# A fused two-block layer on one core: the last two expert steps written out, and the order of work at the seam behind them

## What is computed

```python
def _expert_ffn(xb, w_gu, b_gu, w_down, b_down):
    gu = xb @ w_gu + b_gu                      # 1024 -> 2048
    gate, up = gu[:, :D_EXPERT], gu[:, D_EXPERT:]
    gate = jnp.minimum(gate, SWIGLU_LIMIT)
    up = jnp.clip(up, -SWIGLU_LIMIT, SWIGLU_LIMIT)
    glu = gate * jax.nn.sigmoid(SWIGLU_ALPHA * gate)
    return ((up + 1.0) * glu) @ w_down + b_down   # 1024 -> 1024
...
x = _layernorm(DEEPNORM_ALPHA * x + moe_out + ple, ln2_g, ln2_b)
# second block
mod = c @ w_ada + b_ada
shift, scale, gate = jnp.split(mod, 3, axis=-1)
h = rmsnorm(x, norm_g) * (1.0 + scale) + shift
proj = h @ w_in          # V0, Q0, K0, V1, ... are its units of 512 columns
```

## Time and profile before

| what | value |
|---|---|
| median of three runs | 1740.6 us |
| the profiled execution | 1739.38 us, span 1737.6 us |
| TensorE busy (records) | 1700.8 us, 98% of the span |
| TensorE weight loads busy | 997.3 us, 57% |
| VectorE busy | 570.5 us, 33% |
| ScalarE busy | 261.1 us, 15% |
| chain that ended last | TensorE 91%, DMA 5%, VectorE 2%, ScalarE 1% |
| data moved | 540.46 MB, mean 311 GB/s |
| mean granted TensorE clock | 0.999 of 2.4 GHz |

### The profile page before, as it was taken

One profiled execution on the slowest core, in us unless ns is written; L12 is line 12 of the kernel. 1 busy time (PEld: TensorE's weight loads), 2 busy tenths in 40 slices (PEclk: granted clock), 3 DMA queues, 4 the chain that ended last, 5 costly groups with the idle time before them and its releaser, 6 DMA issues.

```text
span 1737.6 us, 24288 instructions
## 1 busy us (share of the span) xinstructions
PE 1700.8 (98%) x10121; PEld 997.3 (57%) x10121; DVE 570.5 (33%) x1070; ACT 261.1 (15%) x446; POOL 28.9 (2%) x42
## 2 busy tenths in 40 slices
PE   8999999999999999999999999999999989999998
PEld 7787888888643433333333333433333338998885
DVE  2784377454341111111111111111121235536603
ACT  0323115002011111101010101101010121112200
POOL 1000000100000000000000000000000000000000
PEclk9999999999999999999999999999999999999999
DMA  8564332545799999999999999999999995532331
GB/s 320 191 257 183 146 122 100 166 164 191 270 404 424 421 424 427 427 427 428 428 427 428 426 428 427 428 428 427 426 428 427 428 418 205 194 146 102 141 143 46
DMA packets 65257, 540.46 MB, mean 311 GB/s; under 512 B 5514, under 2 KB 14276, under 8 KB 35744
## 3 DMA queue, kind: packets, MB, share of 16 engines
q1 hardware_dynamic: 58464, 527.31, 74.0%
q10 hardware_dynamic: 4560, 5.90, 1.2%
q0 software_dynamic: 2160, 6.17, 1.1%
HBM read 533.57 MB, written 5.78 MB: 310 GB/s over the span
## 4 chain that ended last, share of the span: by engine, by line
PE 91%; DMA 5%; DVE 2%; ACT 1%; issue 1%; SPq 0%; DVEq 0%; ACTq 0%
PE small L1440 24%; PE small L1482 12%; PE proj L816 10%; PE proj L1590 6%; PE proj L1002 5%; DMA arena<-in_expert_w_gu 4%; PE proj L1666 4%; PE proj L1415 3%; PE small L1388 3%; PE small L1427 2%; PE small L1447 2%; PE small L1081 2%; PE small L837 2%; PE proj L826 2%; PE proj L1529 2%; PE small L1547 2%
## 5 line engine op out<-in xcount | busy, mean ns | idle before, releaser
L1440 PE MATMUL small<-arena 128*64 128x512 f32 x2048 | 447.1, 593 | 6.8 <-DMA arena<-in_expert_w_gu 4.3
L1440 PEld LDWEIGHTS small<-arena 128*64 128x64 f32 x2048 | 151.1, 137 | 287.4 <-issue 274.5
L1482 PE MATMUL small<-arena 128*64 128x512 f32 x1024 | 226.8, 595 | 8.6 <-ACT arena L1924 7.9
L2593 DVE TENSOR_SCALAR arena<-small 128x512 f32<-128x512 f32 x32 | 22.1, 692 | 544.3 <-PE small L1447 544.3
L816 PE MATMUL proj<-arena 128*128 128x256 f32 x832 | 183.2, 380 | 0.9 <-DMA arena<-in_w_in_first 0.9
L816 PEld LDWEIGHTS proj<-arena 128*128 128x128 f32 x832 | 157.0, 190 | 23.1 <-DMA arena<-in_w_in_first 1.3
L1482 PEld LDWEIGHTS small<-arena 128*64 128x64 f32 x1024 | 74.5, 137 | 138.8 <-issue 138.8
L1590 PE MATMUL proj<-arena 128*128 128x128 f32 x896 | 100.5, 275 | 0.5 <-ACT arena L1982 0.5
L1590 PEld LDWEIGHTS proj<-arena 128*128 128x128 f32 x896 | 100.3, 192 | 1.1 <-ACT arena L1982 0.7
L1749 ACT ACTIVATE arena<-proj 128x512 f32<-128x512 f32 (+2 forms) x76 | 43.7, 593 | 361.1 <-PE proj L816 118.4
L1920 ACT ACTIVATE arena<-arena 128x512 f32<-128x512 f32 x32 | 20.1, 629 | 495.0 <-DVE arena L2593 495.0
(11 more groups left out here) (455 smaller groups left out, 1576.6 us busy)
## 6 DMA issues: line engine op xcount, KB each, us to landing
arena<-in_expert_w_gu SPq DMA_DIRECT2D x128, 2048.0 KB, 20.6
arena<-in_expert_w_down SPq DMA_DIRECT2D x31, 2048.0 KB, 28.0
arena<-in_expert_w_down SPq DMA_DIRECT2D x33, 1536.0 KB, 30.3
arena<-in_w_in_first SPq DMA_DIRECT2D x20, 2048.0 KB, 8.5
arena<-in_w_in SPq DMA_DIRECT2D x16, 2048.0 KB, 7.3
arena<-in_expert_w_down SPq DMA_DIRECT2D x33, 512.0 KB, 19.8
arena<-in_w_ada SPq DMA_DIRECT2D x6, 2048.0 KB, 9.9
arena<-in_w_branch SPq DMA_DIRECT2D x4, 2048.0 KB, 8.2
```

The source lines that it names most:

```text
L1440: mm = pe.matmul(bank[CAP * half:CAP * half + CAP, :], XG[:, k % 4, k // 4, :], w[:, k % 4, n * D + half * W:n * D + half * W + W], start= ...
L1482: mm = pe.matmul(y_bank[CAP * half:CAP * half + CAP, :], HM[:, m, u, :], w[:, half * W:half * W + W], start=u == 0 and m == 0, stop=u == 1 ...
```

## The change

The loop over expert steps ends two steps earlier on every engine, and its bounds n_steps - 2 and n_steps - 3 are computed into `total` and loaded into registers. The last two steps, a and b = a + 1 (30 and 31), are written out. SyncE issues both steps' gate/up weights, then both steps' down weights. TensorE does step a up to the turning of the rows, the gate/up product of b, the down product of a, turning of h of b, scatter of a, turning of b's slots, the down product of b. Step b has no gather and no turned rows. Its h is copied to the place of XG, its y is built in another bank.

At the seam "ada rows 5" moves from ahead of the first transposes to between H 0 and V0 0; "ada 4", "ada 5" and "gate8" move behind V0 1. The V0 weights are loaded in four pieces of 0.5 MB (chunks m and m + 4 of eight), each with a semaphore that V0 0 waits for piece by piece, and V0 0 sums its pairs in a slightly different nesting. ScalarE does the layer norm's root ahead of the copy of ada rows 4, and the copy of ada rows 5 behind the modulation of H 0. VectorE adds ada 4 and 5 behind the modulation of h 1. The helpers `gate_and_up`, `slots_turned`, `h_turned`, `down` hold what stood in TensorE's `expert_step`; the counts of unit semaphores are adapted to V0's own semaphores.

```diff
          + [f"Wb A {i}" for i in range(4)] + ["mix 0", "mix 1", "mix 2", "x1 0 0", "x1 0 1", "mix 3"]
          + ["logits 0", "x1 1 0", "x1 1 1", "logits 1", "rank", "gateT", "picked", "xg"]
-         + ["ada rows 4", "ada rows 5", "ada 4", "ada 5", "h 0", "h 1", "gate8"]
+         + ["ada rows 4", "h 0", "ada rows 5", "h 1", "ada 4", "ada 5", "gate8"]
          + [x for p in range(HEADS // 2) for x in [f"T {2 * p + odd} {b}" for odd in range(2) for b in range(3)] + [f"O {p}"]]
          + ["pool 0", "pool 1"]
          + [f"{n} {i}" for n in ("Wb2a", "Wb2p") for i in range(4)] + [f"mix2 {i}" for i in range(5)])
...
+            before_two = sp.value_load(total[0:1, 2:3], min_val=EXPERTS - 3, max_val=EXPERTS * T // CAP - 3)
@@ -699,9 +701,21 @@
                     expert_rows(3, u, half)
-            with sp.Fori(4, n_steps, 2) as i:
+            with sp.Fori(4, before_two + 1, 2) as i:
                 expert_block(i, False)
                 expert_block(i + 1, True)
+            for odd in range(2):
+                for u in range(2):
+                    for half in range(2):
+                        sp.wait_ge(sig("gu_used"), 4 * before_two + (4 * odd + 2 * u + half + 1))
+                        expert_rows(EXPERTS - 2 + odd, u, half)
+            for odd in range(2):
+                sp.wait_ge(sig("down_used"), before_two + odd)
+                down_first(EXPERTS - 2 + odd, odd)
+                sp.wait_ge(sig("y_full"), before_two + odd)
+                down_second(EXPERTS - 2 + odd, odd, slice(0, 3))
+                sp.wait_ge(sig("y_full"), before_two + (odd + 1))
+                down_second(EXPERTS - 2 + odd, odd, slice(3, 4))
             for i in range(2):
                 sp.wait_ge(sig("gu_used"), 4 * n_steps)
                 half = ins["w_ada_2"][0, :, (4 + i) * W:(5 + i) * W]
...
@@ -717,6 +731,10 @@
+                if n == 0:
+                    for m in range(4):
+                        sp.dma_start(weights2(name)[:, m::4, :], unit2_source(name)[0][:, m::4, :]).then_inc(sig(f"first_in_{m}"), 16)
+                    continue
                 sp.dma_start(weights2(name), unit2_source(name)[0]).then_inc(sig(f"unit2_in_{n % 3}"), 16)
...
                     mm = pe.matmul(x_bank[:, 0:P], XT[:, k, j * P:j * P + P], PLEW[:, k, bass.ds((i % 8) * P, P)], start=k == 0, stop=k == KD - 1)
                 mm.then_inc(sig("ple_full"), 1)
 
-            def expert_step(i, tile, odd, before=None):
...
@@ -1457,33 +1511,14 @@
                 if tile is not None:
                     pe.wait_ge(sig("ple_sig"), i - 7)
                 gather(x_bank).then_inc(sig("gathered"), 1)
-                pe.wait_ge(sig("pickw_ready"), i + 1)
-                for j in range(TT):
-                    mm = pe.transpose(y_bank[:, j * P:j * P + P], PICKW[:, j, :], ident)
-                mm.then_inc(sig("ptw_full"), 1)
-                pe.wait_ge(sig("h_ready"), i + 1)
-                for m in range(4):
-                    mm = pe.transpose(gate_bank[:, m * P:m * P + P], GH.rearrange("s (p k) -> s p k", k=4)[:, :, m], ident)
-                mm.then_inc(sig("ht_full"), 1)
+                slots_turned(i, y_bank)
+                h_turned(i)
                 pe.wait_ge(sig("rows_ready"), i + 1)
                 turn_rows(up_bank).then_inc(sig("rows_turned"), 1)
-                pe.wait_ge(sig("ptw_ready"), i + 2)
-                pe.wait_ge(sig("hm_ready"), i + 1)
-                for u in range(2):
-                    if odd:
-                        pe.wait_ge(sig(f"odd_in_{2 + u}"), 16 * i + 16 if u else 8 * i + 24)
...
-                    for m in range(4):
-                        w = expert_room(2 + u)[:, m, :]
-                        if odd and 4 * u + m < 7:
-                            w = extra[:, m, :] if u else more[:, m, :]
-                        for half in range(2):
...
@@ -1504,11 +1539,25 @@
+            before_last = pe.value_load(total[0:1, 1:2], min_val=EXPERTS - 2, max_val=EXPERTS * T // CAP - 2)
             two_steps(24, 26, None)
             pe.wait_ge(sig("ple_mul"), 18)
             for j in range(TT):
                 expert_bias(j)
-            two_steps(26, n_steps, None)
+            two_steps(26, before_last, None)
+            a, b = before_last, before_last + 1
+            expert_step(a, None, False, down_now=False)
+            pe.wait_ge(sig("hm_ready"), a + 1)
+            gate_and_up(b)
+            pe.wait_ge(sig("ptw_ready"), a + 2)
+            down(a, False, y_bank, HM)
+            h_turned(b)
+            pe.wait_ge(sig("y_ready"), b)
+            scatter()
+            slots_turned(b, up_bank)
+            pe.wait_ge(sig("hm_ready"), b + 1)
+            down(b, True, x_bank, HM_LAST)
+            pe.wait_ge(sig("ptw_ready"), b + 2)
             pe.wait_ge(sig("last_y_ready"), 1)
             for j in range(TT):
                 scatter((j,), counted=True)
...
-            pe.wait_ge(sig("seam_ready"), 1)
-            for i in range(2):
+            def ada_rows2(i):
+
...
+            pe.wait_ge(sig("seam_ready"), 1)
+            ada_rows2(0)
+            pe.wait_ge(sig("seam_ready"), 2)
+            w = weights2("V0")
+            for j in range(TT):
+                pe.wait_ge(sig("x2n_done"), j + 1)
+                for ps, lo, full_ in ((small(f"h {j}"), 0, "small_full"), (proj(f"H {j}"), 4, "proj_full")):
+                    for m in range(4):
+                        mm = pe.transpose(ps[:, m * P:m * P + P], base[:, j, (lo + m) * P:(lo + m + 1) * P], ident)
+                    mm.then_inc(sig(full_), 1)
+                if j == 0:
+                    ada_rows2(1)
+                ps = proj(f"V0 {j}")
+                for m in range(4):
+                    if j == 0:
+                        pe.wait_ge(sig(f"first_in_{m}"), 48)
+                    for k, piece in ((m, "h_low"), (4 + m, "h_high")):
+                        pe.wait_ge(sig(piece), 4 * j + m + 1)
+                        mm = pe.matmul(ps[:, :], HT[:, k, j * P:j * P + P], w[:, k, :], start=m == 0 and k == 0, stop=m == 3 and k > 3)
+                mm.then_inc(sig("proj_full"), 1)
             pe.wait_ge(sig("small_out"), small_no("ada rows 5") + 1)
             for i in range(2):
                 ps = small(f"ada {4 + i}")
                 for m in range(4):
                     mm = pe.matmul(ps[:, m:m + 1], ADAROW2[:, i, m * P:m * P + P], SEL2, start=True, stop=True)
                 mm.then_inc(sig("small_full"), 1)
-            pe.wait_ge(sig("seam_ready"), 2)
-            for j in range(TT):
-                pe.wait_ge(sig("x2n_done"), j + 1)
-                for ps, lo, full_ in ((small(f"h {j}"), 0, "small_full"), (proj(f"H {j}"), 4, "proj_full")):
-                    for m in range(4):
-                        mm = pe.transpose(ps[:, m * P:m * P + P], base[:, j, (lo + m) * P:(lo + m + 1) * P], ident)
-                    mm.then_inc(sig(full_), 1)
-                if j == 1:
-                    pe.wait_ge(sig("small_out"), small_no("ada 5") + 1)
-                    pe.transpose(small("gate8")[0:8, 0:P], MODT[:, 16:24], ident).then_inc(sig("small_full"), 1)
-                w = unit2("V0")
...
+            pe.wait_ge(sig("small_out"), small_no("ada 5") + 1)
+            pe.transpose(small("gate8")[0:8, 0:P], MODT[:, 16:24], ident).then_inc(sig("small_full"), 1)
...
@@ -1937,8 +2004,15 @@
                 expert_step(i, True)
             act.wait_ge(sig("total_ready"), 1)
             n_steps = act.value_load(total[0:1, 0:1], min_val=EXPERTS, max_val=EXPERTS * T // CAP)
-            with act.Fori(24, n_steps) as i:
+            before_last = act.value_load(total[0:1, 1:2], min_val=EXPERTS - 2, max_val=EXPERTS * T // CAP - 2)
+            with act.Fori(24, before_last) as i:
                 expert_step(i, False)
+            a, b = before_last, before_last + 1
+            expert_step(a, False, down_now=False)
+            sigmoid_of_gate(b)
+            y_copied(a, y_bank)
+            h_copied(b, HM_LAST)
+            y_copied(b, x_bank)
             act.wait_ge(sig("y_ready"), n_steps)
             act.nop().then_inc(sig("last_y_ready"), 1)
...
@@ -1962,14 +2036,15 @@
+                act.wait_ge(sig("small_out"), n)
                 act.activation(ADAROW2[:, i, :], small_bank[n % 4][:, :], ACT.Copy).then_inc(sig("small_out"), 1)
 
             log_and_exp()
+            rsqrt(rs2[:, 0:1], "ln2_var", "ln2_rstd", 1)
             ada_rows2(0)
-            rsqrt(rs2[:, 0:1], "ln2_var", "ln2_rstd", 1)
-            ada_rows2(1)
             squares_of_x2(0)
             modulated(0)
+            ada_rows2(1)
             rsqrt(rs2[:, 1:2], "ln2_var", "ln2_rstd", 2)
             squares_of_x2(1)
...
@@ -2573,7 +2650,7 @@
-                dve.wait_ge(sig("gathered"), i + 1)
-                pick(PICK, nxt, "pick_ready", False)
+                if not last:
+                    dve.wait_ge(sig("gathered"), i + 1)
...
```

(21 more changed lines are left out.)

82 lines of the change are left out of this document (57 added, 25 removed).

## The result

| | before | changed |
|---|---|---|
| median (range) of eight runs each, same chip, us | 1739.76 (1738.69 to 1742.21) | 1746.54 (1745.22 to 1750.49) |
| ratio changed / before, with its 95% interval | | 1.0041 [1.0032, 1.0050] |
| profiled execution, us | 1739.38 | 1750.49 |
| its span, us; mean granted clock | 1737.6; 0.999 | 1748.7; 0.993 |
| start of the run of Q0, K0 and the rest | 1447.58 | 1451.64 |

The profiled execution was the slowest of its eight. It already lies 2.0 us behind at the expert bias of step 30 (1378.06, before 1376.07), and its first expert step has a gate/up product of 15.65 us instead of 13.95, under a low clock; whether that is all of the 2.0 us is not shown.

A forecast was written before the change was run, and what follows sets the result against it. TensorE, busy 98% of the span, was taken as the bound, with loads setting the pace near the loop's end. Terms -3.6 + 1.4 + 2.4 + 3.9 = +4.1 us gave 1744.7 as a median; range 1741.5 to 1748.5.

The forecast's parts named there:

- rival 1: Seam: new 3.85 us idleness before the run's third product brings a second low clock, +1.5, in all +5.6, 1746.2; 17%.
- the case that I held likeliest: Whole kernel: the forecast itself, slower by +3 to +5 us, with 52%.
- Part 1: Last two expert steps: load waits, a gather and transposes go, so the last down product ends 3.6 us sooner.
- I take it as unbroken: Expert loop's end: the load stream has no gap near 1372, with 8 us in hand.
- the down weights of 31 end at 1411.7 as before: Step 31: reordered transfers leave the landing time of its down weights unchanged.
- Rival 2: Step 31: the down product follows the last landing, -6.6 instead of -3.6, sum +1.1, 1741.7; 9%.
- Part 2: Seam's first half: "ada rows 5" moves from idle time onto the path, +1.4 net.
- the -0.2 for the root: Seam: taking the layer norm's root ahead of the ada copy starts the first transposes 0.2 us sooner.
- Part 3: Seam's second half: columns and gate row on the path, +2.4; third product waits for VectorE's sums, +3.9.
- the V0 pieces cost nothing: Seam: cutting the V0 load is worth nothing, as its weights land before V0 is wanted.
- The second register load: Expert loop: a second register load on each engine costs nothing, falling before 1372 where TensorE has time to lose.
- Rival 3: Seam: the low clock falls wholly into the first idle time, so the sum is +2.7, 1743.3; 14%.

The follow-up runs named there:

- changed_again: The changed kernel run once more with no edit: 1748.0 us, 1.0041 of the kernel before.
- Experiment 7: Changed kernel with the last 0.5 MB of step 31's down weights loaded to a free place without waiting: 1747.54 us, 1.0042 of the kernel before.
- columns_behind: Changed kernel with ada 4 and 5 columns behind the run's second product and the gate row behind its first unit: 1740.74 us, 1.0004 of the kernel before.
- filler_both: Changed kernel with 20 identity products ahead of the first transposes and 16 ahead of the run's third product: 1744.46 us, 1.0020 of the kernel before.
- experiment 6: Changed kernel with V0's weights in one load instead of four pieces: 1750.12 us, 1.0049 of the kernel before.
- experiment 3: The same run as columns_behind: changed kernel with columns and gate row moved behind the run's first products, 1740.74 us.
- rows5_ahead: Changed kernel with "ada rows 5" back ahead of the first transposes and its copy ahead of the squares: 1748.46 us, 1.0045 of the kernel before.
- experiment 1: The same run as loop_alone: only the last two expert steps changed, the seam as before, 1740.81 us.
- kept_busy: Changed kernel with Experiment 7's load, ada 4 columns and 14 identity products before the transposes, ada 5 and gate row behind units 0 and 1: 1737.82 us.
- loop_alone: Changed kernel with everything behind the expert loop undone, so only the last two steps differ from before: 1740.81 us, 1.0004 of the kernel before.
- experiment 12: Kernel before the change with four identity products ahead of the first transposes: 1739.51 us, 0.9995 of the kernel before.
- v0_in_one: The same run as experiment 6: changed kernel with V0's weights in one load, 1750.12 us.

## Why the prediction was right in sign and short in size

The sign and the range held (1746.5 within 1741.5 to 1748.5); the difference was +6.8 where +4.1 was forecast. What came about is rival 1, at 17%, whose time was 1746.2, and not the case that I held likeliest. That 1746.2 and 1746.5 nearly agree is luck in part. The forecast was added to 1740.6, the median of three runs, and eight runs gave 1739.8; as a difference rival 1 said +5.6, and the medians say +6.8 to +7.4, the profile of `changed_again` +8.6. No miss made up for another: every term of the sum came out as forecast or worse.

**Part 1, -3.6, measured -2.5 to -2.8.** The removed waits, the gather and the transposes went as counted, and "I take it as unbroken" held: the stream ran at 429 and 433 GB/s in 1365 to 1375, and the last gate/up quarter landed at 1392.1, forecast 1392.0. In `changed_again`, 0.10 us later than before at the bias, three small terms were off by 0.8 together. Gate/up of 31 started at 1383.37, 0.15 later than counted; the down product of step 30 took 7.41 us instead of 7.09, waiting for weights where I had no wait (0.77 us in one piece in the other profile); the last half waited 0.52, where I counted 0.2. The step that failed is "the down weights of 31 end at 1411.7 as before". SyncE may issue their last 0.5 MB only when step 30's down product has ended, and the change moves that end behind the gate/up product of step 31: from 1389.9 to 1405.7. SyncE waits 26.6 us for it, the piece lands 7.1 us behind its issue, at 1412.8, and the stream runs at 328 GB/s in 1405 to 1410, before at 400. Experiment 7, in which that piece does not wait, had 408 and 387 GB/s and no wait in the last product; its 0.3 to 0.5 us are within the noise of the times. Rival 2 is out: the product started behind TensorE's own work, and only its second half waited for a load.

**Part 2, +1.4, measured +2.3.** The mechanism is the predicted one and one length was off. The clock was low from the first transposes to the end of "ada rows 5" instead of for 3.0 us: 3.49 us for that product (3.64 in the other profile) where I counted 2.5. Of the -0.2 for the root 0.1 came: the transposes start 10.0 us behind the last down product, before 10.1. In `columns_behind`, where the low stretch was short, the term was +1.4; in `filler_both`, where there was none, -0.2. I had written down that the longer idle time could lengthen the stretch, as an addition to rival 1, and left it out of the sum. That the V0 pieces cost nothing is in line with experiment 6. The second register load was not tried by itself; in `changed_again` the bias of step 30 stands 0.1 us later than before.

**Part 3, +2.4 and +3.9, measured +6.3.** Both terms came as worked out: 3.88 us idle where 3.85 were forecast, ended by VectorE's weight sums, and experiment 3 takes them away together by moving the columns in the queues. This part carries the result: without the wait and the low clock behind it (experiment 3, where the 1.84 us of the columns stay) the change measures 1740.7, no different from before.

**Rival 1.** I priced the second stretch at +1.5 from the length of the old one; it was +2.7 to +2.9, since it was about twice as long: the clock rose again at some 1462.3 in `changed_again` and 1465.0 in the other profile, so 5.3 and 5.6 us of work ran at half speed. I gave it 17% because the trace showed an idle 1.57 us without a fall. That row was 2.5 times shorter than the gap in question, and the idle times of the old seam, shorter still, had brought one. The Trainium skill, "TensorE: Matmul & The Clock Gate", section "Why this matters for your kernels", made rival 1 the likelier outcome; the runs agree: behind the seam's unfilled idle times of 3.5 us and more work ran at low clock in every profile (in `rows5_ahead` from some 0.5 us behind it on), and behind the filled ones at 1.00. It ran at low clock behind some shorter ones too: 1.11 us in the kernel before, 2.44 and 2.25 us in `rows5_ahead`. Why it did is not shown.

**Rival 3** (the low stretch falls into the idle time) came in no profile.

**What the gain came to.** The loop's end is worth 2.5 to 2.8 us at its own end and nothing that the times show by itself (experiment 1), as the seam behind it was held by a load that the new order of issues made later, and by a longer low stretch. `kept_busy` lets some of it through: by its interval 0.7 to 3.8 us under the kernel before.

## What to carry to other kernels

Work moved ahead of a run on one engine must be followed through the queue of the engine that answers it: eight products of 1.84 us, moved, cost 6.3 us, and 3.9 of these because VectorE, in order, had the sums for a later product behind them. An idle time that a change makes on TensorE is to be priced with the low clock behind it, here 2.5 to 2.9 us behind 3.9 us idle, and can be filled with products whose result nobody reads. And where a stage is made to end sooner, look at the load that the next stage waits for, and at what its issue waits for: an order that is better for one engine moved the end of a product that SyncE waits for by 16 us, and the load that the seam waits for landed 1.5 us later (`loop_alone`).

## What the runs showed that I had not expected

- The low clock lasted longer than in the old seam: 1428 to 1434 and 1459 to 1465 at 0.50 throughout, against some 3 us of work before. In `columns_behind` the same 5.32 us of idleness brought a shorter stretch (0.71 over 1429 to 1432, 1.00 over the next 3 us). In `loop_alone` the product "ada rows 5", behind 2.55 us of idleness, took 1.92 us, at full clock; in `rows5_ahead` the same product behind 2.44 us took 3.17, with the clock at 0.50 over 1426 to 1429. The length of the idle time alone does not tell. What decides stays open.
- Identity products of 128 x 128, over 3.4 or 4.7 of the 5.3 us and 3.7 of the 3.9, kept 2.4 GHz. How little filling is enough was not tried beyond the four products of experiment 12.
- In `rows5_ahead` the first two products of the run, behind V0 1 at full clock, the columns and 0.33 us of idleness, took 5.43 us, with the clock at 0.50 over 1454 to 1456. In the seven other profiles with the same sequence they took 3.80, at full clock. Why it fell in this one is open.

```profile
1449.82 1.84 PE L1632 MATMUL small<-arena 128*128 128x1 f32 x16
1451.99 0.27 PE L1635 MATMUL small<-arena 128*8 128x128 f32 x1 [0.33 <-DVE arena L2162]
1452.10 5.43 PE L1643 MATMUL proj<-arena 128*128 128x128 f32 x32
1459.78 5.44 PE L1643 MATMUL proj<-arena 128*128 128x128 f32 x32 [2.25 <-DVE arena L2768]
```

- Three of the twelve profiles of kernels with new code (the changed kernel's first, `columns_behind` and `v0_in_one`) have one more low stretch 900 us earlier, in the first expert step, where TensorE waits 0.89 us for the router: 15.65 us for 64 products instead of 13.95. The two profiles with the old code do not have it. It may make up much of the changed kernel's wider range (5.3 us against 3.5 before). Why it comes in some runs only, and whether the old kernel is free of it, is open.
